# A decoder layer's weights laid out for long DMA runs, and more window copies issued by ScalarE

## The reference, cut to what matters

```
mod = silu(c) @ w_ada + b_ada                       # w_ada 1024 x 6144: six vectors of 1024 for each c
sh1, sc1, gt1, sh2, sc2, gt2 = split(mod, 6)
h = rmsnorm(x) * (1 + sc1) + sh1
qa, ka, va, fa, qb, kb, vb = split(h @ w_in)        # 512 columns each, fa 8
oa, ob = attend(...)                                # forgetting attention; dilated windows
x = x + gt1 * (concat(rmsnorm(oa), rmsnorm(ob)) @ w_o)      # w_o 1024 x 1024
h2 = rmsnorm(x) * (1 + sc2) + sh2
x = x + gt2 * moe(h2)                               # router, 64 experts, 8 for each token, and a shared one
# an expert: (silu(h2 @ w_gate) * (h2 @ w_up) * gate) @ w_down; w_gate, w_up 1024 x 256, w_down 256 x 1024
ek = concat([buf_k, k_new], axis=1); return ek[:, 1:]       # the window buffers of the samples, moved by one row
```

## Time and profile before

| | us |
|---|---|
| median of 3 runs | 1496.65 (1496.37 to 1498.79) |
| profiled execution | 1504.03 |
| its span | 1502.3 |
| TensorE busy | 1272.7 (85%) |
| VectorE busy | 488.6 (33%) |
| ScalarE busy | 266.7 (18%) |
| GpSimd busy | 244.6 (16%) |
| time of q1's packets (138,608, 349.55 MB), share of 16 DMA engines | 64.6% |
| of q0's (28,576, 89.10 MB) | 20.5% |
| of q10's (5,040, 22.06 MB) | 4.8% |

### The profile page before, as it was taken

How to read it: one execution, slowest core, us unless ns; L and a number is a source line. 1 busy time by engine, 2 the same in 40 slices (tenths; PEclk the granted TensorE clock), 3 DMA queues, 4 the chain that set the end, 5 groups by cost and what they waited for, 6 DMA issues and landing times.

```text
span 1502.3 us, 17576 instructions
## 1 busy us (share of the span) xinstructions
PE 1272.7 (85%) x5908; PEld 647.8 (43%) x5908; DVE 488.6 (33%) x1400; ACT 266.7 (18%) x599; POOL 244.6 (16%) x284
## 2 busy tenths in 40 slices
PE   4997899837787878788989999999899999989980
PEld 1775664314343434344434444444344444434430
DVE  2363544033443422215432222222122222222213
ACT  2221110112232234011001111111111111111110
POOL 1200000122333300000012222222122122212210
PEclk9999999968888889988999999999999999999995
DMA  9999999898989758177359999999999999999964
GB/s 356 371 336 345 354 342 341 252 371 315 390 284 383 256 199 327 42 237 255 126 193 327 334 350 363 361 356 346 360 339 336 360 339 353 351 340 357 327 198 128
DMA packets 172315, 461.85 MB, mean 307 GB/s; under 512 B 13232, under 2 KB 14512, under 8 KB 172096
## 3 DMA queue, kind: packets, MB, share of 16 engines
q1 hardware_dynamic: 138608, 349.55, 64.6%
q0 software_dynamic: 28576, 89.10, 20.5%
q10 hardware_dynamic: 5040, 22.06, 4.8%
HBM read 431.89 MB, written 106.07 MB: 358 GB/s over the span
## 4 chain that ended last, share of the span: by engine, by line
PE 65%; DMA 14%; SPq 7%; DVE 6%; issue 5%; ACT 3%; POOL 0%; POOLq 0%; DVEq 0%; ACTq 0%
PE banks L681 21%; PE banks L705 11%; PE banks L1517 6%; PE banks L537 5%; PE banks L1507 4%; DMA reg_w<-in_w_ada 4%; DMA routed_sum<-reg_w,sidx 3%; DMA reg_w<-h_rows,gidx 3%; PE banks L582 2%; SPq L1365 2%; SPq L1366 2%; PE banks L1689 1%; PE banks L690 1%; PE banks L603 1%; DMA reg_q<-in_cache_k 1%
## 5 line engine op out<-in xcount | busy, mean ns | idle before, releaser
L681 PE MATMUL banks<-reg_q,reg_w 128*128 128x512 f32 (+1 forms) x768 | 313.9, 628 | 21.1 <-issue 17.8
L681 PEld LDWEIGHTS banks<-reg_q,reg_w 128*128 128x128 f32 (+1 forms) x768 | 121.8, 177 | 188.4 <-issue 188.4
L705 PE MATMUL banks<-reg_q,reg_w 128*128 128x512 f32 (+1 forms) x384 | 154.8, 603 | 8.7 <-ACT reg_w L1199 8.7
L1298 POOL DMA_INDIRECT routed_sum<-reg_w,sidx x64 | 97.2, 1518 | 306.6 <-DMA routed_sum<-reg_w,sidx 163.7
L1055 DVE SCALAR_TENSOR_TENSOR reg_w<-banks,small,reg_w 128x256 f32<-128x256 f32 x52 | 25.1, 483 | 342.4 <-ACT reg_w L1194 342.4
L1294 POOL DMA_INDIRECT reg_w<-h_rows,gidx x52 | 55.2, 1062 | 455.6 <-DVE gidx L1015 423.7
L681 PE MATMUL banks<-hT,reg_w 128*128 128x512 f32 (+1 forms) x256 | 122.3, 634 | 6.9 <-issue 6.9
L1194 ACT ACTIVATE reg_w<-banks 128x256 f32<-128x256 f32 x52 | 19.9, 384 | 464.5 <-PE banks L681 464.5
L1517 PE MATMUL banks<-hT,reg_q 128*128 128x260 f32 x384 | 89.1, 392 | 2.4 <-DVE hT L1773 1.6
L1067 DVE COPY reg_w<-banks 128x512 f32<-128x512 f32 x52 | 35.9, 691 | 163.2 <-PE banks L705 163.2
L705 PEld LDWEIGHTS banks<-reg_q,reg_w 128*128 128x128 f32 (+1 forms) x384 | 55.6, 170 | 70.2 <-issue 58.5
(11 more groups left out here) (371 smaller groups left out, 1456.2 us busy)
## 6 DMA issues: line engine op xcount, KB each, us to landing
reg_q<-in_w_gate_up SPq DMA_DIRECT2D x48, 2048.0 KB, 20.6
reg_q<-in_w_down SPq DMA_DIRECT2D x48, 1024.0 KB, 22.9
hT<-in_w_gate_up SPq DMA_DIRECT2D x16, 2048.0 KB, 26.3
out_win_k_s<-in_win_k SPq DMA_DIRECT2D x8, 4094.0 KB, 38.6
reg_w<-in_w_ada SPq DMA_DIRECT2D x11, 2048.0 KB, 26.5
reg_w<-in_w_down SPq DMA_DIRECT2D x16, 1024.0 KB
out_win_v_s<-in_win_v SPq DMA_DIRECT2D x4, 4094.0 KB, 36.0
out_win_v_s<-in_win_v ACTq DMA_DIRECT2D x4, 4094.0 KB, 18.5
```

Of the source, the lines that this page charges most:

```text
L681: last = mm(pb[j % 2][of, :], lhsT=xT[:, j % 2, k, of], rhs=wgu[LOAD[p] % 4][:, k, :], start=(k == 0), stop=(k == KC - 1))
L705: last = mm(pb[6 + hh][of, :], lhsT=aT[:, j % 2, c, of], rhs=wdn[LOAD[p] % 4][:, c, hh * 512:hh * 512 + 512], start=(c == 0), stop=(c == 1))
L1298: nc.gpsimd.indirect_dma_start(rsum, bass.IndirectOffsetOnAxis(ap=idx[0:of.stop - of.start, :], axis=0), y[of, u, :], None, bounds_check=T ...
```

## The change

First, the host lays w_ada, w_in, w_o, w_gate_up, w_down, ws_gate_up and ws_down out so that what a load brings to one partition is contiguous: 16 KB for the 2-MB loads, 8 KB for w_down and ws_down. What lands in the buffers is the same, and so are the bytes, the loads' number and order. Second, NLATE is 8: SyncE issues eight copies in the projection stage, at other steps, and ScalarE eight in the output projection, rounded up by tile: 2, 2, 1, 2, 1 where it had 0, 1, 1, 1, 1.

```diff
--- before.py
+++ after.py
@@ -128,7 +128,7 @@
-NLATE = 4
+NLATE = 8
...
@@ -413,8 +413,6 @@
         pv_ready, oT_copied, rl_set = sem("pv_ready"), sem("oT_copied"), sem("rl_set")
-
-        win_cols = [0, W, 3 * W + H, 4 * W + H, 2 * W, 5 * W + H]
...
@@ -1149,7 +1147,7 @@
                       ACT.Copy).then_inc(h2T_set, 1)
-                for n in range(2 * NS - NLATE + t * NLATE // TT, 2 * NS - NLATE + (t + 1) * NLATE // TT):
+                for n in range(2 * NS - NLATE - (-t * NLATE // TT), 2 * NS - NLATE - (-(t + 1) * NLATE // TT)):
                     copy_window(act, n, late_out)
...
@@ -1214,16 +1212,15 @@
             for s in range(2):
-                sp.dma_start(wslot[s], I["w_o"][:, s * 512:s * 512 + 512].rearrange("(k p) n -> p k n", p=P)
-                             ).then_inc(group_in[s], 16)
+                sp.dma_start(wslot[s].rearrange("p a b -> p (a b)"), I["w_o"][s]).then_inc(group_in[s], 16)
             sp.dma_start(xres[:, :], I["x"][0:P, :]).then_inc(xres_in, 16)
-            sp.dma_start(wslot[2], I["ws_gate_up"].rearrange("(k p) n -> p k n", p=P)).then_inc(group_in[2], 16)
+            sp.dma_start(wslot[2].rearrange("p a b -> p (a b)"), I["ws_gate_up"]).then_inc(group_in[2], 16)
...
             def load_gu(u, w):
-                sp.dma_start(wgu[u], w.rearrange("(k p) n -> p k n", p=P)).then_inc(wgu_in[u], 16)
+                sp.dma_start(wgu[u].rearrange("p a b -> p (a b)"), w).then_inc(wgu_in[u], 16)
...
             def load_dn(u, w):
-                sp.dma_start(wdn[u], w.rearrange("(c p) n -> p c n", p=P)).then_inc(wdn_in[u], 16)
+                sp.dma_start(wdn[u].rearrange("p a b -> p (a b)"), w).then_inc(wdn_in[u], 16)
...
@@ -1237,7 +1234,7 @@
             sp.wait_ge(proj_ready, 2 * TT)
-            sp.dma_start(wsd, I["ws_down"].rearrange("(c p) n -> p c n", p=P)).then_inc(wsd_in, 16)
+            sp.dma_start(wsd.rearrange("p a b -> p (a b)"), I["ws_down"]).then_inc(wsd_in, 16)
             sp.wait_ge(x1_set, 2 * TT)
...
@@ -1252,9 +1249,9 @@
                 sp.wait_ge(gu_ready, freed + 1)
-                load_gu(n % 4, I["w_gate_up"][ds(expert, 1), :, :].rearrange("a k n -> (a k) n"))
+                load_gu(n % 4, I["w_gate_up"][ds(expert, 1), :, :].rearrange("a p n -> (a p) n"))
                 sp.wait_ge(y_ready, 2 * freed + 2)
-                load_dn(n % 4, I["w_down"][ds(expert, 1), :, :].rearrange("a k n -> (a k) n"))
+                load_dn(n % 4, I["w_down"][ds(expert, 1), :, :].rearrange("a p n -> (a p) n"))
             sp.wait_ge(m_over, 1)
...
@@ -1262,9 +1259,9 @@
                         sp.wait_ge(oh_set, i * NE + (NU + 1 + p))
-                        sp.dma_start(wgu[0], I["w_gate_up"][ds(expert, 1), :, :].rearrange("a (k p) n -> (a p) k n", p=P)
+                        sp.dma_start(wgu[0].rearrange("p a b -> p (a b)"), I["w_gate_up"][ds(expert, 1), :, :].rearrange("a p n -> (a p) n")
                                      ).then_inc(m_in, 16)
-                        sp.dma_start(wdn[0], I["w_down"][ds(expert, 1), :, :].rearrange("a (c p) n -> (a p) c n", p=P)
+                        sp.dma_start(wdn[0].rearrange("p a b -> p (a b)"), I["w_down"][ds(expert, 1), :, :].rearrange("a p n -> (a p) n")
                                      ).then_inc(m_in, 16)
...
@@ -1406,9 +1403,7 @@
                 b = BUFFER[which, n]
-                at = 512 * n if which == "ada" else win_cols[n]
-                sp.dma_start(wslot[b], I["w_" + which][:, at:at + 512].rearrange("(k p) n -> p k n", p=P)
-                             ).then_inc(group_in[b], 16)
+                sp.dma_start(wslot[b].rearrange("p a b -> p (a b)"), I["w_" + which][n]).then_inc(group_in[b], 16)
...
@@ -2134,6 +2129,14 @@
     cols = lambda g: g.reshape(KC, P).T
+
+    def tiled(w, starts, n):
+
+        lead = w.shape[:-2]
+        w = w.reshape(lead + (-1, P, w.shape[-1]))
+        return c(np.stack([np.moveaxis(w[..., s:s + n], -2, -3).reshape(lead + (P, -1)) for s in starts]))
+
+    win_cols = [0, W, 3 * W + H, 4 * W + H, 2 * W, 5 * W + H]
     both = lambda g: np.concatenate([g, g])
...
@@ -2147,15 +2150,16 @@
         "x": c(np.concatenate([a["x_prompt"][0], a["x_sample"][:, 0]])),
-        "w_ada": a["w_ada"][0], "w_in": a["w_in"][0],
+        "w_ada": tiled(a["w_ada"][0], range(0, 6 * D, 512), 512), "w_in": tiled(a["w_in"][0], win_cols, 512),
         "cache_k": c(cache_k.reshape(NPHYS, P, W)), "cache_v": c(a["cache_v_a"][0][:, ::-1].reshape(NPHYS, PAGE, W)),
...
         "win_k_seen": c(wk), "win_v_seen": c(wv),
-        "w_o": a["w_o"][0], "w_router": c(a["w_router"][0].reshape(KC, P, NE).transpose(1, 0, 2)),
-        "w_gate_up": c(np.concatenate([a["w_gate"][0], a["w_up"][0]], -1)), "w_down": a["w_down"][0],
-        "ws_gate_up": c(np.concatenate([a["ws_gate"][0], a["ws_up"][0]], -1)), "ws_down": a["ws_down"][0],
+        "w_o": tiled(a["w_o"][0], (0, 512), 512), "w_router": c(a["w_router"][0].reshape(KC, P, NE).transpose(1, 0, 2)),
+        "w_gate_up": tiled(np.concatenate([a["w_gate"][0], a["w_up"][0]], -1), (0,), 2 * F)[0], "w_down": tiled(a["w_down"][0], (0,), D)[0],
+        "ws_gate_up": tiled(np.concatenate([a["ws_gate"][0], a["ws_up"][0]], -1), (0,), 2 * F)[0],
+        "ws_down": tiled(a["ws_down"][0], (0,), D)[0],
     }
...
```

## The result

The changed kernel takes 1572.77 us (median of 4 runs, 1572.1 to 1576.93) against 1496.51 for the kernel before: 1.0513 times as long, 95% interval 1.0491 to 1.0535. That is **76 us slower**; the forecast was slower by 36. The execution that the profile shows took 1572.1 us, its span is 1570.4, 68.1 more than the span before; the other 8 us between 68 and 76 lie in the profiled execution of before, which was itself 7.5 above its median.

A forecast was written before the change was run, and what follows sets the result against it. TensorE was taken to set the pace nearly everywhere, DMA close behind in the experts. Experts +33, front -2, output projection +5 make +36 on 1504.03, 1540 profiled, scaled by 0.9951 to 1532 us; range 1460 to 1575.

The forecast's parts named there:

- Prices of packets: Experts' weight loads: 16-KB packets cost 0.62 us, 8-KB 0.32; each expert's loads take 0.5 us less of each DMA engine.
- Rival D: Experts' loads: a 16-KB packet costs 1.12 us, not 0.62, giving a time above 1800 us; chance 0.03.
- Turns: Experts: queues alternate single packets, so each gather or scatter row waits 0.37 us more; 16 turns make 6.0, taken as 5.4.
- zero slack: Experts, behind a pair: the gather lands just when TensorE wants its rows, at 940.2 us, so any delay is waited for.
- The slow matmuls behind a wait: Experts: after waiting for the gather, TensorE's matmuls run slower, adding 1.8 us a period.
- The front: Program's start: x's lateness costs +6.4 us, the vanished w_ada wait at 129.72 saves 8.5; taken as -2 together.
- The output projection: Output projection: ScalarE's eight late copies, one perhaps blocked 13.15 us by a full queue, cost +5, between 0 and +9.
- The baseline: Whole kernel: the profiled 1504.03 us plus 36 gives 1540, scaled by 0.9951 to the median.
- B: Whole kernel faster: turns grow but nobody is late, or long packets are split; about -30, 1467 us; chance 0.29.
- C: Whole kernel unchanged within 0.2%: late gathers and cheaper loads cancel in the experts; 1496 us; chance 0.07.
- E: Experts' loads: engines get 2-KB pieces all the same, so times stay; no chance of its own, counted under C.
- The upper case: Experts: the scatters' own chain, five a period, becomes the bound at 59.8 us a period, +58 us.

The follow-up runs named there:

- dose8: Kernel before with only the experts' and shared expert's weights laid out in longer runs, experts' packets kept at 8 KB: 1545.2 us, ratio 1.0297.
- experts_warm12: Kernel before with experts' and shared expert's weights in 16- and 8-KB runs, plus 12 idle matmuls a pair on TensorE: 1537.7 us, ratio 1.0265.
- front_only: Kernel before with only w_ada, w_in and w_o in 16-KB runs: 1505.2 us, ratio 1.0039.
- layout_only: Kernel before with all of the changed layout but four late copies as before: 1569.2 us, ratio 1.0447.
- dose4: Kernel before with only experts' and shared expert's weights relaid, gaps between runs keeping experts' packets at 4 KB: 1481.8 us, ratio 0.9890.
- after_early: Changed kernel with GpSimd issuing the gather ahead of a pair's second scatter: 1524.4 us, ratio 1.0166 to the kernel before.

## Why the prediction was right in sign and wrong in size

**Prices of packets: right.** 16 KB were put at 0.62 us and 8 KB at 0.32, drawn on from packets of up to 10 KB. In the changed kernel's trace, while the gather behind the pair at 998 us was in flight (1010.6 to 1021.6), 166 packets of 16 KB took 0.615 us each on average and 136 of 8 KB 0.310. Rival D (1.12 us) is out.

**Turns: the sum right, partly by luck, the rule behind it not.** "One packet each, whatever its size", read from three queues at the start of the program, doesn't hold in the experts. While the gather was in flight, before (932 to 940 us) and after (1010.6 to 1021.6), the two queues moved:

```profile
q1 hardware_dynamic: 985, 2.35, 76.5%
q0 software_dynamic: 224, 0.63, 27.9%
```

```profile
q1 hardware_dynamic: 346, 3.83, 82.3%
q0 software_dynamic: 224, 0.61, 19.9%
```

Without packets of 4 bytes these are 965 to 153 and 302 to 148: the loads got 6.3 packets through for one row of GpSimd's before and 2.0 after. Nor does the rule hold for GpSimd's plain loads beside 2-KB packets (38 to 43 us before: 135 packets of q0 to 708 of q1). It does hold for such loads beside the 8-KB packets of a window copy, at 227 to 231 us before:

```profile
q1 hardware_dynamic: 127, 0.97, 64.9%
q0 software_dynamic: 128, 0.45, 32.8%
```

The 10.4 us of the earlier trace rows, from just before, do not show longer turns, though: the first of these loads was issued at 221.61, and until 225 us q0 moved no packet at all.

In the experts a row of q0 took each engine 8.0 x 16/153 = 0.84 us before and 11.0 x 16/148 = 1.19 after, 0.35 more, close to the 0.37 forecast. One reading is a time of its own between two rows, and on top of it one packet of the other queue; that is an inference, and the sizes between do not bear it out. The first scatter of a pair lands on average after 7.5, 7.5, 8.9 and 10.1 us with packets of 2 and 4, 4, 8, and 16 and 8 KB, and the gather behind it after 8.2, 8.2, 10.3 and 11.1 (the first as in the earlier trace rows), where one packet more for each of its eight rows would add 0.5, 1.3 and 1.2 step by step. What law the delay follows stays open. The sum was 6.0 for sixteen turns: 2.7 us for the first scatter (forecast 1.5) and 2.9 for the gather's landing behind the second (forecast 4.5) make 5.6, so two errors cancel. With zero slack (right: TensorE is ready 17.9 us behind the pair in both traces) the wait was put at 5.4 and is 64.8/11 = 5.9 a period.

**The slow matmuls behind a wait: the term that failed.** The step "behind a wait I add the slow matmuls, 8.78 - 7.02 = 1.8" took the first 32 matmuls behind one wait and stopped there. Behind the gather's wait the slow stretch is longer: 1.97 - 1.04 at L666, 0.89 - 0.67 at L654 and 5.60 - 3.70 at L703, together 3.1 here; over the eleven waits L703 takes 6.0 on average, which makes it 3.4. By the periods (59.7 - 50.3 - 5.9) it is 3.5, and 3.7 in dose8, where the wait is only 3.8. Filling the wait took it away (experts_warm12). Over eleven periods that is 1.7 x 11 = 19 us of the missing 27 in the experts; the wait, 0.5 x 11, gives 5 more. The last 3 us are the other side of the period before: 54.5 was the mean over ten periods, over all eleven it is 54.2.

**The front: the term with the wrong middle.** The forecast had both parts, x later by 8.7 (measured 9.2) and the wait at 129.72 gone (so it was), and let them add to -2. It is +4.5 at 140 us of the trace, +0.4% in front_only. The step missed what the late x sets off: TensorE stood idle for 3.97 and 6.52 us and then ran its next pieces slowly (the granted clock is 0.50 from 22 to 49 us, the lower level throughout, and was 1.00 from 29 to 44 us before). The turning of x, 6.34 us in the earlier trace rows, took 1.29 + 8.99, and the 16 matmuls of the third w_ada group 3.64 in place of 1.93: 11.7 us at the first projection instead of 6.4. It is the same failing as in the experts.

**The output projection: the size about right, the mechanism not.** +5 was taken; from 590 us to the first expert the lag grows by 4.6, of which layout_only, with four late copies, has 0.8. But ScalarE was never blocked for 13 us: its five issues took 1.41 (two copies), 1.33 (two), 0.58, 1.31 (two) and 1.36, and the sigmoid still waited for TensorE. How the copies cost TensorE those 4 us is not shown. A copy that met a full queue had held SyncE for 13.15, but that queue was full of 2-KB packets. With long ones SyncE's own issues are short, also behind the first three (0.33 to 0.49 us for each group, where most took 2.5 to 13.5 before):

```profile
1.79 2.33 SPq L1406 DMA_DIRECT2D reg_w<-in_w_ada  x3
```

**A misread column.** "DMA share 0.96" in the last two thirds of the experts is the granted clock; the share is 0.99. DMA was even closer behind TensorE than the prediction says; nothing was worked out from the 0.96.

**The baseline.** The forecast scaled the profiled execution of before (1504.03) by 0.9951 to the median. The growth by spans is 68 us, by medians 76. That execution was slower than the median by 7.5 us and the one after was not, so the forecast's scaling took off 7 us that the result then showed again.

**Rivals.** B (turns stay short) fell with the first trace: the waits are there. But half of its arithmetic was sound, as dose4 shows: loads in fewer packets are a gain (17 us at 4 KB, where 27 were put down for 16) wherever the turns stay short. C and E did not come. The upper case, the scatters' own chain as the bound (59.8 a period), happens to have the right number (59.7) for a wrong reason: GpSimd's third scatter of the period still waited for VectorE's copy, not for a landing (issued at 1044.58 in the changed kernel, released by L1065), and experts_warm12 made the period shorter without touching the scatters.

## What to carry to other kernels

When a load is laid out in longer runs, look first at what shares the DMA engines with it through another queue and is waited for with no slack; here 4 KB was the size that made the loads cheaper and left gathers and scatters of 4-KB rows alone, and 16 KB cost 4%. Price a new wait of TensorE by its own length plus what its matmuls take longer behind it: some 3.5 us each here behind waits of 3 to 7 us, and some 1 us on average behind the waits of about 2 us that after_early has. A small input that the first stage needs belongs ahead of the large loads, in their own queue; that was tried only beside loads in 16-KB runs.
